# A ring of weight tiles in SBUF, filled by transfers of two tiles (1 MB) instead of one (512 KB)

## The reference, cut to what matters

```python
def swiglu(x, w_gu, w_down):
    g, u = jnp.split(x @ w_gu, 2, axis=-1)
    return (jax.nn.silu(g) * u) @ w_down

h = h + MACARON_SCALE * rms_norm(swiglu(rms_norm(h, ffn1_pre_g), ffn1_w_gu, ffn1_w_down), ffn1_post_g)
h = h + rms_norm(hybrid_mixer(rms_norm(h, mix_pre_g), ..., w_in, ..., w_out), mix_post_g)
h = h + MACARON_SCALE * rms_norm(swiglu(rms_norm(h, ffn2_pre_g), ffn2_w_gu, ffn2_w_down), ffn2_post_g)
for l in range(2):
    proj = rmsnorm(h, norm_g[l]) @ w_in[l]          # 1024 x N_IN, and w_uq, w_ukv for the latent attention
    ...
    merged = g_a * (y_a @ w_out_a[l]) + g_b * (y_b @ w_out_b[l]) + g_c * (y_c @ w_out_c[l])
    h = h + merged @ w_o[l]
```

## The time and the profile before

| | |
|---|---|
| median of three runs | 1307.19 us (1307.13 to 1307.91) |
| the profiled execution | 1307.46 us; its span 1305.7 us, 1.8 us outside it |
| PE busy (matmuls) | 1296.2 us, 99% |
| DVE busy | 896.2 us, 69% |
| ACT busy | 709.0 us, 54% |
| DMA, queue q1 of the sync engine | 62064 packets, 224.42 MB, 53.9% of 16 engines |
| raw<-weights | 422 transfers of 512 KB, 4.1 us in the median from issue to landing |

### The profile page before, as it was taken

One profiled execution on the slowest core, in us unless ns is written; L12 is line 12 of the kernel. 1 busy time (PEld: TensorE's weight loads), 2 busy tenths in 40 slices (PEclk: granted clock), 3 DMA queues, 4 the chain that ended last, 5 costly groups with the idle time before them and its releaser, 6 DMA issues.

```text
span 1305.7 us, 18174 instructions
## 1 busy us (share of the span) xinstructions
PE 1296.2 (99%) x7332; PEld 1102.1 (84%) x7332; DVE 896.2 (69%) x1032; ACT 709.0 (54%) x976; POOL 87.1 (7%) x77
## 2 busy tenths in 40 slices
PE   9999999999999999999999999999999999999999
PEld 7788888987778888888888999888888889998887
DVE  6756556687978755547667567856776766687575
ACT  7544445568746544435766544544467665445451
POOL 0000000000001000000252000000012610000000
PEclk9999999999999999999999999999999999999999
DMA  9866637542376766554665544465656564345562
GB/s 323 270 210 205 204 104 253 166 127 83 130 253 212 263 191 185 187 162 145 190 198 177 175 133 129 143 197 177 195 185 220 172 213 146 105 138 163 176 192 84
DMA packets 64963, 234.42 MB, mean 180 GB/s; under 512 B 7664, under 2 KB 7792, under 8 KB 64752
## 3 DMA queue, kind: packets, MB, share of 16 engines
q1 hardware_dynamic: 62064, 224.42, 53.9%
q10 hardware_dynamic: 2816, 8.84, 1.9%
HBM read 232.19 MB, written 1.05 MB: 179 GB/s over the span
## 4 chain that ended last, share of the span: by engine, by line
PE 90%; DVE 5%; DMA 2%; ACT 2%; issue 1%; POOL 0%; SPq 0%; ACTq 0%; another core or an unknown queue 0%; POOLq 0%; DVEq 0%
PE psum L1923 22%; PE psum L1944 22%; PE psum L1924 22%; PE psum L1929 5%; PE psum L1976 5%; PE psum L1930 5%; PE psum L1991 5%; DMA raw<-weights 2%; PE psum L2124 2%; DVE w_lo L1181 1%; PE psum L2378 1%; DVE y_lo L1181 1%; PE psum L2224 1%; PE psum L2364 0%; ACT y_hi L602 0%
## 5 line engine op out<-in xcount | busy, mean ns | idle before, releaser
L1181 DVE TENSOR_TENSOR w_lo<-raw,w_hi 128x1024 fp32r<-128x1024 f32 x226 | 274.1, 1221 | 136.8 <-ACT w_hi L602 135.3
L602 ACT ACTIVATE w_hi<-raw 128x1024 fp32r<-128x1024 f32 x226 | 237.7, 1056 | 150.7 <-PE psum L1944 115.1
L1181 DVE TENSOR_TENSOR y_lo<-raw,y_hi 128x1024 fp32r<-128x1024 f32 x144 | 175.3, 1221 | 65.9 <-ACT y_hi L602 65.1
L1923 PE MATMUL psum<-w_hi,x_hi 128*128 128x512 f32 x552 | 217.7, 394 | 1.0 <-ACT w_hi L602 1.0
L1924 PE MATMUL psum<-w_hi,x_lo 128*128 128x512 f32 x552 | 214.6, 389 | 0.0
L602 ACT ACTIVATE y_hi<-raw 128x1024 fp32r<-128x1024 f32 x144 | 151.9, 1056 | 84.6 <-PE psum L1944 57.1
L1944 PE MATMUL psum<-w_lo,x_hi 128*128 128x512 f32 x552 | 170.0, 389 | 0.0
L1923 PE MATMUL psum<-y_hi,x_hi 128*128 128x512 f32 (+1 forms) x376 | 148.2, 394 | 0.4 <-DVE arena L1262 0.4
L1924 PE MATMUL psum<-y_hi,x_lo 128*128 128x512 f32 (+1 forms) x376 | 146.3, 389 | 0.0
L1923 PEld LDWEIGHTS psum<-w_hi,x_hi 128*128 128x128 f32 x552 | 103.8, 188 | 23.7 <-issue 3.0
L1944 PEld LDWEIGHTS psum<-w_lo,x_hi 128*128 128x128 f32 x552 | 103.7, 188 | 21.8 <-DVE w_lo L1181 0.4
(11 more groups left out here) (207 smaller groups left out, 2270.5 us busy)
## 6 DMA issues: line engine op xcount, KB each, us to landing
raw<-weights SPq DMA_DIRECT2D x422, 512.0 KB, 4.1
arena<-gains ACTq DMA_DIRECT2D x7, 512.0 KB, 4.9
arena<-gate_bias ACTq DMA_DIRECT2D x2, 1536.0 KB, 7.5
norm<-x_feat SPq DMA_DIRECT2D x4, 256.0 KB, 5.4
res<-x SPq DMA_DIRECT2D x2, 512.0 KB, 8.9
arena<-lru_w ACTq DMA_DIRECT2D x1, 1024.0 KB, 5.4
cst<-consts ACTq DMA_DIRECT2D x1, 736.0 KB, 5.4
out<-res SPq DMA_DIRECT2D x1, 512.0 KB, 2.6
```

What stands on the lines that cost most here:

```text
L602: act.activation(slot(t)[0], raw[:, t % RAW, :], ACT.Copy).then_inc(hi_ready, 1)
L1181: dve.tensor_tensor(lo, raw[:, t % RAW, :], hi.bitcast(F32), ALU.subtract).then_inc(lo_ready, 1)
L1923: pe.matmul(out_, l_hi, r_hi, start=start, stop=False, skip_group_check=skip)
```

## The change

From tile 4 on the sync engine loads two tiles with one transfer of 1 MB, into places 0 and 1 or 2 and 3 of the ring, once both places are free. The first four tiles are still loaded singly, each with a semaphore of its own. There is one semaphore for each half of the ring. ACT waits for the semaphore of the half in which its tile lies; the splits, their order, the slots and the ring's size are as before.

```diff
-        raw_loaded = [sem(f"raw_loaded{i}") for i in range(RAW)]
+        raw_loaded = [sem(f"raw_loaded{i}") for i in range(RAW // 2)]
+        first_loaded = [sem(f"first_loaded{i}") for i in range(RAW)]
...
             for t in range(ALL_TILES):
                 if t < KD // 2:
                     sp.dma_start(first_pair(t), x_feat[t, :, :]).then_inc(feat_loaded[t], 16)
-                if t >= RAW:
-                    sp.wait_ge(lo_ready, t - RAW + 1)
-                sp.dma_start(raw[:, t % RAW, :], weights[t, :, :]).then_inc(raw_loaded[t % RAW], 16)
+                at = t % RAW
+                if t < RAW:
+                    sp.dma_start(raw[:, at, :], weights[t, :, :]).then_inc(first_loaded[t], 16)
+                elif t % 2 == 0:
+                    sp.wait_ge(lo_ready, t - RAW + 2)
+                    sp.dma_start(raw[:, at:at + 2, :], weights[t:t + 2, :, :].rearrange("t p n -> p t n")
+                                 ).then_inc(raw_loaded[at // 2], 16)
                 if t == 3:
...
-                act.wait_ge(raw_loaded[t % RAW], 16 * (t // RAW + 1))
+                if t < RAW:
+                    act.wait_ge(first_loaded[t], 16)
+                else:
+                    act.wait_ge(raw_loaded[t % RAW // 2], 16 * (t // RAW))
                 act.activation(slot(t)[0], raw[:, t % RAW, :], ACT.Copy).then_inc(hi_ready, 1)
```

## The result

The changed kernel takes 1360.8 us in the median of four runs (1358.2 to 1362.6), against 1307.45 (1307.13 to 1307.91) for the kernel before: a ratio of 1.0406, 95% interval 1.0394 to 1.0419. It is 53 us slower. The sign was forecast; the time, 1343, was not, and 1360.8 lies above the range.

What follows compares the result with a forecast made beforehand. TensorE was taken as the bound (busy 1296.2 of 1305.7 us), with the four-place ring, not DMA, holding loads back. Late-tile terms summed to 35.7 us, giving 1343 us; range 1324 to 1358.

Steps and rivals of the forecast that it cites:

- What bounds the kernel: Whole kernel: PE busy 1296.2 of 1305.7 us; ring short only at the start and changes of stage; steady parts lose 0.
- L = 5.2 us: Ring loads from tile 4 on: a 1 MB transfer takes 5.2 us from issue to landing, range 4.8 to 5.8.
- The round of the build-up: Start of the kernel: four tiles cost 8.7 us per round where singles took 7.0, adding 6.4 us.
- MIX: Attention of the MIX stage: late pairs add 0.2 us.
- MIX to FFN2: Change of stage: successive pairs land later, delaying a norm and a swish, 9.1 us in all.
- Layer 0 to 1: Change of layer: pairs (308,309) and (318,319) come late, costing 3.0 and 1.4, together 4.4 us.
- The clock: Rival: after six gaps of PE the clock falls, slowing one tile each, adding 16 us: 1359; chance 0.08.
- matmuls of 0.78 us: Sign given for the lower clock: matmuls in the new profile would take 0.78 us.
- Hidden: Rival: bigger transfers land as early as singles, so no loss or a gain, 1305.7 to 1307; chance 0.05.
- Partly made good: Rival: at changes of stage the ring runs ahead while PE stands, so 36 falls to about 22: 1329; chance 0.16.
- The ring as the bound in the steady parts: Rival: from L of about 6.5 us each swish waits for its tiles, also in FFN steps: 1386; chance 0.05.

Runs made afterwards that it cites:

- the first fillers: Changed kernel with short identity matmuls ahead of five of PE's waits (FFN1, FFN2, dilated heads of the layers): 1353.5 us, ratio 1.0346.
- the fillers: Changed kernel with identity matmuls ahead of the first five waits, plus the third swish of FFN1 and MIX's merged branches: 1349.9 us, ratio 1.0312.
- The run at a clock of 1.000: One of the four runs of the changed kernel with identity matmuls at all filled places, including the two added later: 1346.6 us.

## Why the prediction was right or wrong

- *What bounds the kernel.* Right: matmuls unchanged, no loss in steady parts (pairs there alone cost nothing measurable), losses at the start and at the changes of stage.
- *L = 5.2 us.* 5.0 was measured in the median, within 4.8 to 5.8. The page of the Trainium skill ("DMA: Bandwidth & Descriptors", "Anatomy of one DMA — SWDGE (gpsimd) path") gives 4.4 for transfers that GpSimd issues; these, from the sync engine, took 5.0, so the figure doesn't hold for them. The rule to batch to 1 MiB for bandwidth (same page of the Trainium skill, "Bandwidth") found nothing to gain, as pairs and singles in a ring of six took the same time.
- *The round of the build-up.* 8.7 forecast, 8.56 to 8.73 measured. The term was 6.4 and became 7.3, because the second pair landed at 20.35 in place of 19.3.
- *MIX.* The term of 0.2 is a step that failed: 3.1 us of waiting and 4.9 in all. I compared the tiles with PE's lead and not with the DVE operations that stand behind them; at all other places I had followed those.
- *MIX to FFN2.* The term was 9.1. The 7.3 us of waiting are partly luck, since one load of 7.49 us is in them and part of the waiting is made up while the clock is low. In the run with the first fillers, where the granted clock was 1.00 from 64 to 639 us and no load of this chain was over 5.3, the shift grew by 8.8 there: the term was right.
- *Layer 0 to 1.* The term of 4.4 was too large: the 3.0 of (308,309) came as 2.5, the 1.4 of (318,319) didn't come. With MIX it nearly cancels, so a sum of idle time that is right to 1.2 us hides two errors of 2 to 3.
- *The clock.* This is the step that made the number wrong: the sum has no term for it. I called it a rival at 0.08 and priced it at 16 us; the granted clock cost 17.7 us by its mean, 18 us of the shift are no wait, and the fillers got 11 us of the 53 back. That the rival's 1359 is close to 1360.8 is partly luck: it counts six gaps at 2.7 us each, where the clock fell at eight gaps and cost 1.3 to 3.0 each. The sign that it named was matmuls of 0.78 us; those at the lower clock took 0.63 and began every 0.43. The only evidence that I had weighed was that gaps up to 1.4 us had left the clock alone, which says nothing of gaps of 4. The Trainium skill ("TensorE: Matmul & The Clock Gate", "HAM oscillation — how this bites in real kernels") tells of waits for data after which TensorE goes on at 1.2 GHz, and the traces here agree: 0.50 in the window behind the gap of 3.87 us.
- *The rivals.* Hidden: no. Partly made good: no, the chained delays came in full. The ring as the bound in the steady parts: no. The range reached to 1358 by leaving out just the top of the clock's case.

What stays open: the sum of the parts. 36 us of waiting were forecast and 34 seen; without any fall of the clock the waits would be some 38 or 39. The run at a clock of 1.000 lies 38 us above the kernel before, and the profiled kernel with all fillers has a shift of 44.0, of which three falls of the clock account for some 5. That the waits are longer without the falls fits with a slow stretch giving the ring time to catch up, but this was not tried by itself.

## What to carry to other kernels

Loading two tiles at once into a ring takes two things from it: the even tile's place is asked for one tile later, and both are usable only when the last byte is down. In a ring of four that is most of its depth; count rounds (landing plus the time until both places are free again) against what the consumer takes at every place where the ring starts empty, and follow everything that stands behind the tiles in a fixed program. Then look at each gap of TensorE of some 2 us and more: where the clock fell behind one, it cost 1.3 to 3 us on top of its length here, and at eight of nine such gaps of the changed kernel it fell.

## What the runs showed of the hardware

After gaps of 3.03, 4.40 and 6.23 us the matmuls lost 1.5, 2.0 and 1.6 us more, and in the changed kernel 1.6 after 1.97 us and 1.3 after 5.17: in these traces the surcharge doesn't grow with the gap. At gaps between 2 and 3.3 us it came in some executions and places and not in others (0.2 us behind 2.77 at 402.5 us and 1.8 behind 2.59 at 970.0 of the same trace, with the first fillers). The scatter of the slower kernels goes with it: of the kernel with singles up to tile 23, the four runs took 1347.6, 1348.8, 1351.3 and 1354.1 us at granted clocks of 0.994, 0.991, 0.990 and 0.988. Matmuls of the identity by itself, put into the gap, kept the clock at 1.00 at every place where they were put (in the two traces with fillers it fell only at gaps without them).
